# Causal mask of a transposed-score attention: from a product on TensorE to a minimum on VectorE

## What is computed

```python
def attend_block(args):                       # mla_attention, 16 heads
    qn, qp, b = args
    q_pos = N_META + b * BLOCK + jnp.arange(BLOCK)
    s = (jnp.einsum('bqhd,bshd->bhqs', qn, k_nope)
         + jnp.einsum('bqhd,bsd->bhqs', qp, k_pe)).astype(jnp.float32)
    s = jnp.where(k_pos[None, :] <= q_pos[:, None], s, NEG_INF)
    p = jax.nn.softmax(s, axis=-1).astype(v.dtype)
    return jnp.einsum('bhqs,bshd->bqhd', p, v)
```

## Time and profile before

| | |
|---|---|
| time, median of 3 runs | 3388.63 us |
| the three runs | 3388.33, 3388.63, 3399.14 us |
| profiled execution: span from first to last instruction | 3393.5 us |
| its own time beside the span | not shown apart |
| mean granted TensorE clock | 0.956 of full speed |
| TensorE / weight loads busy | 3126.6 us (92%) / 2484.2 us (73%) |
| VectorE / ScalarE / GpSimd busy | 1687.2 us (50%) / 1242.9 us (37%) / 1821.2 us (54%) |
| `attention_b` in the span | about 1649 to 2600 us |

### The profile page before, as it was taken

How to read it: one execution, slowest core, us unless ns; L and a number is a source line. 1 busy time by engine, 2 the same in 40 slices (tenths; PEclk the granted TensorE clock), 3 DMA queues, 4 the chain that set the end, 5 groups by cost and what they waited for, 6 DMA issues and landing times. The chain is left out here.

```text
span 3393.5 us, 56800 instructions
## 1 busy us (share of the span) xinstructions
PE 3126.6 (92%) x19621; PEld 2484.2 (73%) x19621; DVE 1687.2 (50%) x4096; ACT 1242.9 (37%) x2675; POOL 1821.2 (54%) x1447
## 2 busy tenths in 40 slices
PE   6999999899599998799799999999998996999992
PEld 4788887688598897799566666666665885899981
DVE  3555556577344333455365556555661564444333
ACT  2444445222123332444244444444442321332233
POOL 2555555244244443344488888888885222444434
PEclk8999999999799999899699999999998997999996
DMA  3001012644599996455602211221112643999986
GB/s 105 27 28 41 29 40 58 216 149 136 195 328 322 319 317 169 123 160 153 158 10 54 51 26 41 54 51 29 39 60 73 205 149 129 341 320 318 313 240 218
DMA packets 359641, 491.69 MB, mean 145 GB/s; under 512 B 87309, under 2 KB 286753, under 8 KB 357144
## 3 DMA queue, kind: packets, MB, share of 16 engines
q1 hardware_dynamic: 326136, 412.83, 38.7%
q0 software_dynamic: 33312, 76.43, 8.8%
HBM read 362.79 MB, written 135.09 MB: 147 GB/s over the span
## 5 line engine op out<-in xcount | busy, mean ns | idle before, releaser
L2185 POOL TENSOR_TENSOR keep_wg<-keep_wg,ab_pT 128x1024 f32<-128x1024 f32 (+2 forms) x320 | 597.9, 1868 | 90.7 <-ACT ab_pT L2219 48.3
L2219 ACT ACTIVATE ab_pT<-ab_S 128x512 f32<-128x512 f32 (+4 forms) x704 | 349.9, 505 | 511.8 <-PE ab_S L2317 253.7
L2246 DVE TENSOR_REDUCE ab_mx<-ab_W 128x2 f32<-128x800 f32 (+1 forms) x224 | 249.7, 1117 | 207.9 <-PE ab_W L2331 203.2
L1337 POOL DMA_INDIRECT scratch_h<-ex_y,ex_prow x65 | 104.5, 1607 | 437.2 <-ACT ex_yr L1370 258.8
L1509 PE MATMUL ex_G<-ex_xT,keep_wg 128*128 128x160 f32 x2080 | 297.3, 302 | 10.5 <-DMA ex_wu<-in_moe_w_up 10.5
L1509 PEld LDWEIGHTS ex_G<-ex_xT,keep_wg 128*128 128x128 f32 x2080 | 288.1, 192 | 12.1 <-DMA ex_wu<-in_moe_w_up 11.3
L1509 PE MATMUL ex_U<-ex_xT,ex_wu 128*128 128x160 f32 x2080 | 293.1, 299 | 0.0
L1509 PEld LDWEIGHTS ex_U<-ex_xT,ex_wu 128*128 128x128 f32 x2080 | 286.1, 190 | 0.0
L2366 PE MATMUL ab_O<-ab_pT,keep_wg 128*64 128x512 f32 (+4 forms) x1408 | 262.8, 515 | 0.0
L350 POOL TENSOR_TENSOR aa_prob<-aa_prob,aa_rden 128x1024 f32<-128x1024 f32 x68 | 127.4, 1894 | 191.6 <-DVE aa_rden L517 191.6
L1382 DVE TENSOR_TENSOR ex_wd_lo<-ex_wd,ex_wd_hi 128x2048 fp32r<-128x2048 f32 x65 | 149.0, 2292 | 160.2 <-ACT ex_wd_hi L1375 160.2
(11 more groups left out here) (325 smaller groups left out, 7954.1 us busy)
## 6 DMA issues: line engine op xcount, KB each, us to landing
keep_wg<-in_moe_w_gate SPq DMA_DIRECT2D x65, 1024.0 KB, 8.0
ex_wu<-in_moe_w_up SPq DMA_DIRECT2D x65, 1024.0 KB, 10.7
ex_wd<-in_moe_w_down SPq DMA_DIRECT2D x65, 1024.0 KB, 12.4
scratch_h<-pr_h SPq DMA_DIRECT2D x33, 512.0 KB, 5.0
scratch_xn<-pr_xn SPq DMA_DIRECT2D x33, 512.0 KB, 2.7
pr_o<-scratch_oT SPq DMA_DIRECT2D x32, 512.0 KB, 4.7
scratch_qT<-pb_qT SPq DMA_DIRECT2D x17, 768.0 KB, 5.2
scratch_oT<-keep_wg SPq DMA_DIRECT2D x17, 512.0 KB, 2.9
```

The costliest lines, as they stand in the source:

```text
L2185: nc.gpsimd.tensor_tensor(to, to, pT[:, U % RING, :, 0:n], ALU.add).then_inc(added, 1)
L2219: nc.scalar.activation(pT[:, U % RING, h, 0:n], S[:, h, 0:n], ACT.Exp, scale=B_SCALE).then_inc(exped, 1)
L2246: nc.vector.reduce_max(mx[:, :, t, c:c + 1].rearrange("p h a -> p (h a)"), W[:, j % 2, :, 0:n], AX.X).then_inc(emptied, 1)
```

## The change

The mask product and its two constants go. In their place VectorE takes, on diagonal units, the minimum of the exponentials and a table `upper` that holds 1e30 where a key is seen and 0 where it isn't, in place in `pT`, over the partly masked columns of both heads. In its queue the minimum of unit U-1 stands at the head of iteration U, ahead of `work[U]`. A new semaphore `bounded` counts the minimums; the add and the value product of a diagonal unit wait for it instead of for the exponentials.

```diff
-        identb = s.sb("identb", [P, P], BF16)
         mask = s.sb("mask", [P, 512])
+        upper = s.sb("upper", [P, P + META])
-        maskT = s.sb("maskT", [P, P + META], BF16)
...
+        def diagonal(U):
+            p, g, b = units[U]
+            return b >= 4 * g
+
+        diagonals = [sum(diagonal(V) for V in range(U + 1)) for U in range(NU)]
...
                 load_first(0)
-                sp.dma_start(identb[:, :], io["identb"]).then_inc(consts, 16)
                 sp.dma_start(mask[:, :], io["mask_b"]).then_inc(masks_in, 16)
                 sp.dma_start(ident[:, :], io["ident"]).then_inc(consts, 16)
-                sp.dma_start(maskT[:, :], io["mask_bT"]).then_inc(consts, 16)
+                sp.dma_start(upper[:, :], io["bound_bT"]).then_inc(masks_in, 16)
...
                 def add(U):
-                    pool.wait_ge(exped, 2 * U + 2)
+                    if diagonal(U):
+                        pool.wait_ge(bounded, diagonals[U])
+                    else:
+                        pool.wait_ge(exped, 2 * U + 2)
...
             def _(dve):
-                dve.wait_ge(masks_in, 16)
+                dve.wait_ge(masks_in, 32)
+                def bound(U):
+                    tri = masked(U)
+                    k = tri.stop - tri.start
+                    dve.wait_ge(exped, 2 * U + 2)
+                    part = pT[:, U % RING, :, 0:k]
+                    nc.vector.tensor_tensor(part, part, upper[:, tri].unsqueeze(1).to_broadcast([P, 2, k]), ALU.min).then_inc(bounded, 1)
...
                 for U in range(-1, NU + 8):
+                    if 1 <= U <= NU and diagonal(U - 1):
+                        bound(U - 1)
                     for job in work[U]:
...
-                        last = nc.tensor.matmul(to, k_lo[p % 2][0:QD, h, kb], q_hi[p % 2][0:QD, h, qs], start=False, stop=not diagonal)
-                        if diagonal:
-                            last = nc.tensor.matmul(S[:, h, 0:tri.stop - tri.start], identb[:, :], maskT[:, tri], start=False, stop=True)
+                        last = nc.tensor.matmul(to, k_lo[p % 2][0:QD, h, kb], q_hi[p % 2][0:QD, h, qs], start=False, stop=True)
...
                     if (p, g) == (0, 0):
-                        pe.wait_ge(consts, 16 * 3)
+                        pe.wait_ge(consts, 16)
...
                 def attend(U):
-                    pe.wait_ge(exped, 2 * U + 2)
+                    if diagonal(U):
+                        pe.wait_ge(bounded, diagonals[U])
+                    else:
+                        pe.wait_ge(exped, 2 * U + 2)
```

More of the change, by code:

```diff
@@ L2035, in attention_b @@
         exped = s.sem("exped")
+        bounded = s.sem("bounded")
         summed = s.sem("summed")
@@ L2299, in score @@
                     p, g, b = units[U]
-                    n, kb, tri = width(U), keys(U), masked(U)
+                    n, kb = width(U), keys(U)
                     at = P * (4 * g + 5) - n
@@ L2309, in score @@
                             pe.wait_ge(moved[g], 32 * moves(p, g))
-                    diagonal = b >= 4 * g
                     for h in range(2):
@@ L2632, in shape_constants @@
         "ident": np.eye(P, dtype=np.float32),
-        "identb": np.eye(P).astype(bf),
         "cs_a": table(HD),
@@ L2637, in shape_constants @@
         "mask_b": np.concatenate([np.zeros((P, 512 - P)), np.where(k <= q, 0, MASKED)], axis=1).astype(np.float32),
-        "mask_bT": np.concatenate([np.where(q <= k, 0, MASKED), np.where((q >= P - META) & (q - (P - META) <= k), 0, MASKED)[:, 0:META]], axis=1).astype(bf),
+        "bound_bT": np.concatenate([np.where(q <= k, -MASKED, 0), np.where((q >= P - META) & (q - (P - META) <= k), -MASKED, 0)[:, 0:META]], axis=1).astype(np.float32),
         "ones_tri": np.concatenate([(q < k).astype(np.float32), np.ones((P, P), np.float32)], axis=1).astype(bf),
```

## The result

The kernel is **slower, by 0.7%**: median 3415.32 us (3413.51 to 3418.63, 4 runs) against 3390.32 us for the kernel before beside it (3388.33 to 3399.14, 4 runs), ratio 1.0071, 95% interval 1.0058 to 1.0083. That is 25.0 us more; 18 had been forecast.

A forecast was written before the change was run, and what follows sets the result against it. GpSimd was taken to bound over two thirds of each period, TensorE a hair behind. Pairs 1 to 6 +16, pair 0 +3, pair 7 -1.5, rounded to +18 on 3388.6, gave 3407 us, range 3384 to 3428.

The forecast's parts named there:

- What bounds the period: Pairs 1 to 6: GpSimd bounds over two thirds of the 112.68 us period, with TensorE a hair behind.
- long stretch: GpSimd's add of unit 16 to that of unit 43, 77.90 us; minimums clipping its starts cost 0.5 us.
- What is removed: 320 mask products at 0.11 us each; only about 8 per pair count, 0.9 us, all in units 3 to 16.
- What is added: 160 minimums on VectorE, 0.42 us for 256 columns, 59 us in all; free as busy time.
- The waits, pairs 1 to 6: Adds and value products of diagonal units wait for minimums: 2.7 us per period, 16 over six periods.
- near end: Units 3 to 16, reciprocal not delayed: unit 11's add 2.4 us late, GpSimd 0.7 late at unit 16.
- Lock as the cause: A minimum meeting a running GpSimd add waits for its end, up to 2.4 us, with all of VectorE's queue.
- Pair 0: First pair: ten minimums on the path, 5 us, less 20 mask products, 2.2: +3, ends -2 and +8.
- Pair 7: Last pair, bound by TensorE alone: gains at most 4.4 us, gives some back; -1.5, ends -4 and +2.
- TensorE as the bound: Rival: TensorE sets the pace throughout and the gain goes through, 3353 us; chance 0.09 with lesser gains beyond 0.3%.
- Absorbed: Rival: VectorE gets its locks at once and transposes aren't late, 0.7 us per period, about 3387 us; chance 0.25.
- VectorE late in the bursts: Rival: in diagonal bursts VectorE falls behind and TensorE waits, 5 us on all eight pairs, about 3430 us; chance 0.14.

The follow-up runs named there:

- 1: Causal mask left out (neither product nor minimum), all else as in the changed kernel: 3440.68 us, ratio 1.0152, with other routing in it.
- 8: Kernel before, mask untouched, with one, two or four of 16 low parts per pair subtracted by VectorE instead of GpSimd: 3384.35, 3381.35, 3407.95 us.
- 2: Changed kernel without mask product or minimum, one scan computed five times more on TensorE in pairs 1 to 7: period 112.2 us in four of five.
- 4: Changed kernel, mask left out, a maximum over the same columns with one SBUF input in the minimum's place: 3451.35 us, ratio 1.0182, other routing.
- first profile: The profiled execution of the kernel before, unchanged, whose rows the prediction used: span 3393.5 us.
- 6: Also written `inner`: changed kernel with the minimum in pairs 1 to 6 alone, pairs 0 and 7 keeping the mask product: 3401.32 us, ratio 1.0037.
- second profile: The kernel before, unchanged, profiled once more: 3386.7 us, span 3384.9.
- filled: Changed kernel with one scan computed four times more on TensorE in pairs 1 to 7: 3412.0 us, ratio 1.0063.

## Why the prediction was right, and where not

- **What bounds the period**: right. GpSimd's closed sum gives pair 6's long stretch within 0.2 us in the runs with at most two parts moved (with four it doesn't: 73.24 for 75.37); 26 products less on TensorE didn't shorten it (1), and relieving GpSimd (8) did.
- **What is removed**: 0.6 us per period in experiments 2 and 4, for 0.9; nothing in the long stretch, as said.
- **What is added**: right. Minimums in free moments took 0.41 and 0.18 us; the lock more than doubled their mean.
- **The waits, pairs 1 to 6**: +2.7 per period forecast, +2.8 measured in four of the periods of pairs 2 to 6 (+1.3 in pair 5), but made up otherwise. At a clock of 1.00 (pair 5) unit 11's add starts 25.96 us after the hand-over; I had 25.9 for the near end and 27.3 for the value taken. There the near end was the right one: short stretch +1.02, near end 0.7, taken 2.2. The other 1.65 us come from TensorE's clock behind the longer hand-over wait, a term that the sum didn't have. I did write that TensorE's idle time before its divide would stay under 3 us (2.10), and took idle time for free. The long stretch gave 0.16 to 0.34 for 0.5. Sum 13.0 (14.0 against the first profile) for 16: right in size, half of it by luck.
- **Lock as the cause**: in pairs 1 to 6 it is the smaller part. "What matters is the lock", I wrote; it costs 0.6 us per period there, the order in VectorE's queue 1.0 and the clock 1.65 where it falls (4, 6). In pair 7, where I gave it nothing, it is most of the loss.
- **Pair 0**: +3 forecast, +0.2 between two profiles with unlike clocks: open. Without product or minimum it was 2.9 us shorter than with the minimum, for the 5 that I gave the minimums.
- **Pair 7**: the step that failed. "TensorE gains at most 4.4 and gives some back", -1.5 with ends -4 and +2; measured +12.2 (+10.65 against the first profile). I had the lock between the weight split and the adds in the earlier trace rows, from this very pair, and did not put the minimum into that queue. There GpSimd has slack as a sum (83 of 105 us busy), but minimums and weight splits, both on VectorE, wait inside GpSimd's adds; adds, scans and transposes come late one by one, and TensorE stands still for 9.65 us, for 2.39, with its clock at the lower level for 13.7 us. Without the lock (4) 9.6 us of it are gone.
- **Rivals**: TensorE as the bound is refuted (1, 8). Absorbed is refuted by the ratio. VectorE late in the bursts did not decide: its sign was there, a scan that waits 1.0 us in unit 43's iteration of each of pairs 1 to 6, but TensorE's scans waited 8.7 us for these reductions in all eight pairs together (ten waits), where the rival needs 5 in each.

The total, 18 for 25: against the second profile pairs 1 to 6 came out 3 below, pair 0 2.8 below, pair 7 13.7 above. So the total lies in the range because errors of both signs stand beside each other.

## What to carry to other kernels

Work taken off an engine that isn't the bound buys idle time, and on TensorE idle time can cost more than it frees: look at the granted clock behind each wait before and after a change. Before moving an operation onto a half-idle engine, write down what stands ahead of it in that queue at each place, the last, irregular round included; a busy share says nothing of that.

## What the runs showed of the hardware that I had not expected

- **TensorE's granted clock around short waits.** Waits of 1.38 to 1.46 us at six hand-overs of the kernel before left it at 1.00. Behind a wait of 2.10 us (changed kernel, pair 6) and inside one of 2.39 us (no mask) it fell, to 0.76 and 0.61 over the next 7 us, part of them at 1.2 GHz, part at 2.4, and a group of 16 products took 3.97 us for 2.27. But the length of one wait doesn't decide: it fell at scan waits of 1.02 to 1.04 us (changed kernel ahead of the hand-overs to pairs 4 and 5, `filled` pairs 3 and 6), and the hand-overs to pair 7 of the changed kernel and to pair 3 of `inner`, with the same wait of 2.10 us, kept it. Why is open. The Trainium skill, "TensorE: Matmul & The Clock Gate", section "Why this matters for your kernels", warns of idle gaps between bursts, but of longer ones than these. The traces agree that idle time costs clock; on the length the measurement decides, and here the clock also fell at single semaphore waits of 1.0 to 2.4 us.
- **Useless products made a kernel's period shorter**, by 1.6 to 2.6 us (112.2 for 113.8 to 114.9) in four of five periods.
- **The lock's price**: minimums of 256 columns took 0.41 us free, 1.26 and 1.90 inside an add, on average over all sizes 0.90 (0.36 for a maximum over the same columns with one SBUF input).
